# Last attention: the lower part of each head's output, formed by VectorE instead of ScalarE and GpSimd

## The chip, the cores and the metric

The kernel runs on one core of one Trainium2 chip. The metric is the device time of one execution, in microseconds; the time before is the median of 3 runs, 1202.19 us. One execution was also taken by the hardware profiler. The engines are TensorE (PE, with PEld for its weight loads), VectorE (DVE), ScalarE (ACT), GpSimd (POOL) and SyncE (SP, which issues the weight transfers).

## The reference, cut to what matters

A tensor of 256 tokens with 1024 features goes through two blocks. The second block's last layer is an attention with 8 heads of 128 features, followed by an output projection and a feed-forward part. With 256 tokens there is one block of keys, so the attention is causal softmax over all tokens:

```
h = h + moba_mixer(h, ...)        # the attention of this text
h = h + conv_ffn_2(h, ...)

def moba_mixer(x, norm_g, w_q, q_norm_g, w_o, kb, vb, kmean, cos, sin):
    q = rope(rmsnorm(rmsnorm(x, norm_g) @ w_q)) * 128 ** -0.5
    l_own = q @ k.T, masked with -inf where key > query
    p = softmax(l_own)
    o = p @ v                       # per head, 128 features
    return o.reshape(b, s, 1024) @ w_o
```

Everything is float32. The large projections must keep nearly the whole of that precision.

## The kernel before, in words

Activations lie with the features on the 128 partitions and the 256 tokens along the row (T = 256, P = 128, KD = 8 blocks of features). A projection in full float32 is replaced by three products of a rounded type (fp32r): each operand x is split into an upper part, x rounded to fp32r, and a lower part, x minus the upper part, also rounded; the product is upper times upper, lower times upper and upper times lower. Tiles seen through the rounded type carry the name `rounded` in the profile, all other tiles in the on-chip memory the name `arena`.

The weights stream through a ring of 8 slots of 8 blocks each. For each slot ScalarE writes the upper part and VectorE the lower part (`split_to`), in an order written out by hand between the other work of each engine. There is no scheduler: every engine has its own program, and semaphores join them. The accumulation banks are used in a fixed order of units; psA holds the projections and the scores of the attention (`as0` to `as7`), psB the small units: the transposed probabilities (`at0` to `at7`) and the outputs of the heads (`ao0` to `ao7`). A unit may only be opened when the unit that used its bank before has been freed (`freed`, `release`).

The last attention, for head h:

- TensorE, `scores(h)`: four products with the causal mask added as a product, into psA.
- VectorE, `a_max(h)`: two row maxima (L2427, L2428), and the negated and scaled maxima (L2430, 128x2).
- ScalarE, `a_exp(h)`: two exponentials (128 and 256 columns), each with a row sum, and the bank of the scores is free.
- VectorE: reciprocal of the sums (L2437), then the probabilities scaled in place (L2439 with 128 columns, L2440 with 256).
- TensorE, `turn(h)`: three transposes into psB (L1185). ScalarE copies them out (128x384).
- TensorE, `values(h)`: two products with the values, the output of the head, 128x256, into psB.
- ScalarE: the upper part `aoH` of the output (rounded<-psB 128x256, semaphore `ao_upper`), then a full copy `ao` of the same bank (arena<-psB 128x256), which frees the bank.
- GpSimd (L1829): `ao` minus `aoH`, in place, rounded: the lower part (semaphore `ao_rest`).

The engines are staggered. TensorE runs turn(h), values(h-1), scores(h+3) for h = 0 to 7. VectorE runs the probabilities of head h and then a_max(h+2). ScalarE runs the copy of the transposes of head h, the exponentials of head h+2, and then the two instructions on the output of head h-1.

After the heads `project_first` forms the first unit of the output projection (`bo0`): for both halves of its bank blocks 0 to 5 of the features first, then blocks 6 and 7. Before the products of block k it waits until the lower part of head k is there. Then come the other projection units and the last feed-forward part.

The helper `tt` of VectorE (L1878) issues every TENSOR_TENSOR, the helper `A` of ScalarE (L1253) every ACTIVATE, and `mm` of TensorE (L483) every product.

Of the kernel before, what the change touches and what calls it, by code (L numbers as in the profile page):

```python
# [21 lines left out]
ALU = mybir.AluOpType  # L22
# [4 lines left out]
T = 256  # L27
# [157 lines left out]
def program(nc, ins, out):  # L185
    ctx = ExitStack()
    with ctx:
# [291 lines left out]
        def _(pe):  # L479
# [75 lines left out]
            def project_first(name, src, wait, per=1):  # L555

                o = open_(name)
                assert state["blk"] == 0
                w = [[], []]
                for m in range(2):  # L560
                    w[m] = [weights(1) for k in range(KD)]
                    if m:
                        state["inc"] = False
                    for k in range(6):
                        if m == 0:
                            ready(pe, wait, k // per + 1)
                        mm3(o[:, m * T:(m + 1) * T], w[m][k], part(src, slice(0, P), k), k == 0 and m == 0, False,
                            shared=True)
                for m in range(2):
                    for k in range(6, KD):  # L570
                        if m == 0:
                            ready(pe, wait, k // per + 1)
                        elif k == 6:
                            state["inc"] = True
                        last = mm3(o[:, m * T:(m + 1) * T], w[m][k], part(src, slice(0, P), k), False, k == KD - 1,
                                   shared=True)
                close(last, name)
# [449 lines left out]
            for u in range(6, 3 * KD):  # L1027
                branch(u)
            project_first("wo0", (mgH, mg), "merged_rest")
            project([f"wo{u}" for u in range(1, 4)], (mgH, mg))  # L1030

            def ffn(f, rms):
# [18 lines left out]
                def first(j):  # L1051

                    if j == 0:
                        project_first(f"up{f}.0", GX[f"f{f}"], f"xg_f{f}")
                        sum_squares(rms, f"f{f}", GQ[f"f{f}"])
# [8 lines left out]

            project_first("lq0", GX["l"], "xg_l")
            sum_squares("r3", "l", GQ["l"])
# [80 lines left out]

            project_first("bq0", GX["b"], "xg_b")
            sum_squares("r5", "b", GQ["b"])
# [47 lines left out]
            for h in range(9):  # L1197
# [4 lines left out]
                if h < 5:  # L1202
                    scores(h + 3)
            project_first("bo0", (aoH, ao), "ao_rest")
            project([f"bo{u}" for u in range(1, 4)], (aoH, ao))
# [6 lines left out]
        def _(act):  # L1212
# [478 lines left out]
            for h in range(9):  # L1691
# [4 lines left out]
                if h:  # L1696
                    o = take(f"ao{h - 1}")[:, 0:T]
                    A(fr(aoH[:, h - 1, :]), o, ACT.Copy).then_inc(sem("ao_upper"), 1)
                    release(A(ao[:, h - 1, :], o, ACT.Copy), f"ao{h - 1}")
            ffn(2, "r6", "f1", ("bo", "x5"))  # L1700
# [5 lines left out]
        def _(pool):  # L1706
# [113 lines left out]
            for x, src in (("q", aq), ("k", ak)):  # L1820
                for u in range(4):
# [3 lines left out]
                    mul(atm[x][:, s, :], src[:, s, :], bc(cosg[x], 2)).then_inc(sem("a_cos"), 1)  # L1825
            for h in range(8):
                pool.wait_ge(*freed(f"ao{h}"))
                ready(pool, "ao_upper", h + 1)
                nc.gpsimd.tensor_tensor(fr(ao[:, h, :]), ao[:, h, :], rd(aoH[:, h, :]), ALU.subtract)\  # L1829
                    .then_inc(sem("ao_rest"), 1)  # L1830
            ffn(2, "x5")
# [3 lines left out]
        def _(dve):  # L1835
# [589 lines left out]
            def a_max(h):  # L2425
# [4 lines left out]
                V.tensor_scalar(small[:, 56 + 2 * h:58 + 2 * h], small[:, 40 + 2 * h:42 + 2 * h], -P ** -0.5,  # L2430
                                None, ALU.mult).then_inc(sem("a_max"), 1)
            a_max(0)
            a_max(1)
            for h in range(8):
# [9 lines left out]
                if h == 1:  # L2444
                    split_to(SLOT_END["bv11"] + 3)
            residual([f"bo{u}" for u in range(4)], "x5", "f2", "f1")
            ffn(2, "r6", "f1", "x_final", None, None)
# [88 lines left out]
```

## Time and profile before

| what | value |
|---|---|
| median of 3 runs (lowest, highest) | 1202.19 us (1202.01, 1202.54) |
| the profiled execution's own time | 1200.83 us |
| its span in the profile | 1198.8 us |
| TensorE busy | 1161.2 us, 97% |
| VectorE busy | 901.7 us, 75% |
| ScalarE busy | 662.6 us, 55% |
| GpSimd busy | 362.9 us, 30% |
| the last attention, from 957.0 to 977.0 us of the span: TensorE busy | 16.01 of 20.00 us |
| the same stretch: VectorE, ScalarE, GpSimd busy | 13.15, 15.17, 5.14 us |
| granted TensorE clock there | 1.00 |

The span begins with the first instruction of the profiled execution and ends with the last; the execution's own time is a little longer. A busy share over the whole span is a mean over stages of different kinds: in the projections TensorE has hardly a gap, in the attention it waits. A row in order of time has the start in the span, the duration, the engine, the line, the operation with its tiles and shapes, and in square brackets the idle time before it with what ended that. Neighbouring rows of one engine may overlap by some hundredths of a microsecond.

### The profile page before, as it was taken

To read this page: it belongs to the slowest core of one execution; us is meant where nothing else is said; L and a number is where in the kernel's file an instruction comes from. 1 tells how busy PE (TensorE), PEld (TensorE's weight loads), DVE (VectorE), ACT (ScalarE), POOL (GpSimd) and SP (SyncE) were. 2 spreads that over 40 slices of the span, in tenths; PEclk is the share of its full clock that TensorE was granted. 3 is DMA by queue.
4 is the path that set the end of the run, shared out by engine and by line. 5 is a ranking of instruction groups with operands and counts; after the bars stand their busy time and mean duration, and the time that the engine had idled before them with its cause. 6 is when DMAs were issued, how large, how long until landed. Compare 5 with 4: busy or idle time off the path is not lost.

```text
span 1198.8 us, 24765 instructions
## 1 busy us (share of the span) xinstructions
PE 1161.2 (97%) x9416; PEld 1074.1 (90%) x9416; DVE 901.7 (75%) x1305; ACT 662.6 (55%) x974; POOL 362.9 (30%) x326
## 2 busy tenths in 40 slices
PE   8999999899999999999999999999999989999998
PEld 8988678889999999989888999998898789999987
DVE  6989674456678888866757898887676768888853
ACT  5686943454445555544557565554455656555631
POOL 6634101000013555312102245550155023555400
PEclk9999999999999999999999999999999999999999
DMA  8644211236556555555432555555554325555551
GB/s 302 217 149 136 88 36 39 72 125 193 181 187 200 178 182 179 177 192 176 159 124 88 191 173 180 176 176 188 183 173 141 124 71 176 176 175 175 180 189 71
DMA packets 53987, 188.77 MB, mean 157 GB/s; under 512 B 6032, under 2 KB 6160, under 8 KB 53520
## 3 DMA queue, kind: packets, MB, share of 16 engines
q1 hardware_dynamic: 52304, 182.47, 46.9%
q10 hardware_dynamic: 1600, 5.12, 1.3%
q8 instruction: 61, 1.00, 0.3%
q14 instruction: 22, 0.18, 0.0%
HBM read 186.52 MB, written 1.05 MB: 156 GB/s over the span
## 4 chain that ended last, share of the span: by engine, by line
PE 78%; DVE 10%; ACT 7%; issue 3%; DMA 1%; POOL 0%; SPq 0%; DVEq 0%; ACTq 0%; POOLq 0%
PE psA L483 70%; PE psB L483 8%; ACT arena L1253 3%; DVE rounded L1878 3%; DVE arena L1881 3%; ACT rounded L1253 2%; DVE arena L1878 2%; ACT L1253 2%; DMA arena<-in_x 1%; DVE arena L2234 0%; DVE rounded L1881 0%; DVE arena L2389 0%; DVE arena L2330 0%; DVE arena L1912 0%; DVE arena L2283 0%
## 5 line engine op out<-in xcount | busy, mean ns | idle before, releaser
L483 PE MATMUL psA<-rounded,rounded 128*128 128x256 f32 (+1 forms) x7440 | 1011.6, 297 | 16.6 <-DVE rounded L1878 14.7
L483 PEld LDWEIGHTS psA<-rounded,rounded 128*128 128x128 f32 x7440 | 954.1, 191 | 67.3 <-issue 13.4
L1878 DVE TENSOR_TENSOR rounded<-arena,rounded 128x1024 fp32r<-128x1024 f32 (+2 forms) x362 | 458.4, 1287 | 71.6 <-ACT rounded L1253 67.8
L1253 ACT ACTIVATE rounded<-arena 128x1024 fp32r<-128x1024 f32 (+2 forms) x444 | 389.3, 922 | 184.3 <-PE psA L483 62.6
L1708 POOL TENSOR_TENSOR arena<-arena 128x256 f32<-128x256 f32 (+1 forms) x121 | 161.4, 1340 | 589.5 <-ACT arena L1253 220.9
L1253 ACT ACTIVATE arena<-arena 128x256 f32<-128x256 f32 (+6 forms) x276 | 145.4, 562 | 187.3 <-DVE arena L1878 135.1
L1881 DVE SCALAR_TENSOR_TENSOR arena<-arena 128x255 f32<-128x255 f32 (+4 forms) x338 | 177.5, 569 | 31.5 <-ACT arena L1253 21.3
L483 PE MATMUL psB<-arena 64*64 64x64 f32 (+9 forms) x1464 | 136.3, 285 | 10.1 <-DVE arena L1878 3.8
L483 PEld LDWEIGHTS psB<-arena 64*64 64x64 f32 (+4 forms) x1464 | 93.8, 152 | 41.8 <-issue 27.0
L1878 DVE TENSOR_TENSOR arena<-arena,psA 128x256 f32<-128x256 f32 (+1 forms) x84 | 38.4, 458 | 68.6 <-PE psA L483 43.4
L1795 POOL TENSOR_TENSOR rounded<-arena,rounded 128x256 f32 (+1 forms) x63 | 86.0, 1365 | 10.0 <-POOL rounded L1793 8.8
L1253 ACT ACTIVATE arena<-psA 128x512 f32<-128x512 f32 (+2 forms) x58 | 28.9, 507 | 82.8 <-PE psA L483 82.4
L1878 DVE TENSOR_TENSOR arena<-psA,arena 128x512 f32<-128x512 f32 x79 | 54.4, 690 | 20.5 <-PE psA L483 20.1
L1878 DVE TENSOR_TENSOR arena<-psB,arena 128x512 f32<-128x512 f32 (+5 forms) x63 | 34.6, 577 | 31.6 <-PE psB L483 30.7
L1253 ACT ACT_TABLE_LOAD x42 | 53.9, 1283 | 2.0 <-PEq L2530 1.2
L1253 ACT ACTIVATE arena<-psB 128x512 f32<-128x512 f32 (+4 forms) x61 | 28.6, 496 | 44.5 <-PE psB L483 40.2
L1881 DVE SCALAR_TENSOR_TENSOR rounded<-arena,rounded 128x256 fp32r<-128x256 f32 x48 | 37.9, 818 | 18.5 <-ACT rounded L1253 18.5
L1878 DVE TENSOR_TENSOR arena<-arena 128x512 f32<-128x512 f32 (+4 forms) x60 | 40.9, 694 | 11.2 <-ACT arena L1253 10.2
L1714 POOL TENSOR_TENSOR rounded<-arena,rounded 128x256 fp32r<-128x256 f32 x24 | 25.3, 1082 | 28.6 <-ACT rounded L1253 28.6
L1723 POOL TENSOR_TENSOR arena<-arena 128x512 f32<-128x512 f32 x21 | 31.6, 1505 | 1.6
L1253 ACT ACTIVATE arena<-psB,arena 128x256 f32<-128x256 f32 (+1 forms) x45 | 23.4, 562 | 15.1 <-PE psB L483 9.8
L1793 POOL CAST rounded<-arena 128x256 f32 (+1 forms) x63 | 29.0, 460 | 8.9 <-POOL arena L1708 8.0
(73 smaller groups left out, 190.9 us busy)
## 6 DMA issues: line engine op xcount, KB each, us to landing
arena<-in_w SPq DMA_DIRECT2D x343, 512.0 KB, 3.5
arena<-in_mem ACTq DMA_DIRECT2D x2, 512.0 KB, 6.4
arena<-in_x ACTq DMA_DIRECT2D x1, 1024.0 KB, 4.9
arena<-in_con ACTq DMA_DIRECT2D x1, 1024.0 KB, 5.9
out<-arena SPq DMA_DIRECT2D x1, 1024.0 KB, 3.9
arena<-in_con ACTq DMA_DIRECT2D x1, 992.0 KB, 5.1
arena<-in_w SPq DMA_DIRECT2D x2, 256.0 KB, 3.2
arena<-in_x SPq DMA_DIRECT2D x2, 256.0 KB, 5.5
```

The costliest lines, as they stand in the source:

```text
L483: ins_ = nc.tensor.matmul(o, l, r, start=start, stop=stop, skip_group_check=shared)
L1253: return nc.scalar.activation(o, i, f, **kw)
L1708: return nc.gpsimd.tensor_tensor(o, a, b, ALU.mult)
L1714: nc.gpsimd.tensor_tensor(fr(x[:, c, :]), x[:, c, :], rd(upper_[:, c, :]), ALU.subtract)\
L1723: nc.gpsimd.tensor_tensor(dst[:, 0:2, :], dst[:, 0:2, :], dst[:, c, :], ALU.add)\
L1793: nc.gpsimd.tensor_copy(hr_, gv[:, j % 2, :]).then_inc(sem("act_part"), 1)
L1795: nc.gpsimd.tensor_tensor(lr_, gv[:, j % 2, :], hi, ALU.subtract)\
L1878: return V.tensor_tensor(o, a, b, op)
L1881: return V.scalar_tensor_tensor(out=o, in0=a, scalar=s, in1=b, op0=op0, op1=op1)
```

## The change

ScalarE's full copy of each head's output goes, and GpSimd's subtraction goes. VectorE gets `ao_rest(h)`: it waits for the head's bank and for ScalarE's upper part, subtracts the upper part from the bank, writes the lower part rounded, and frees the bank. It stands in the loop over the heads at the end of turn h for head h-2, from h = 2 on, and twice behind the loop. `project_first` now takes a function that gives semaphore and value; for this projection it is the release of the head's bank, for the other three the same waits as before.

```
@@ project_first (TensorE)
-                            ready(pe, wait, k // per + 1)
+                            pe.wait_ge(*wait(k))
...
-            project_first("bo0", (aoH, ao), "ao_rest")
+            project_first("bo0", (aoH, ao), lambda k: freed(f"ao{k}"))
@@ ScalarE, loop over the heads
                 if h:
                     o = take(f"ao{h - 1}")[:, 0:T]
                     A(fr(aoH[:, h - 1, :]), o, ACT.Copy).then_inc(sem("ao_upper"), 1)
-                    release(A(ao[:, h - 1, :], o, ACT.Copy), f"ao{h - 1}")
@@ GpSimd
-            for h in range(8):
-                pool.wait_ge(*freed(f"ao{h}"))
-                ready(pool, "ao_upper", h + 1)
-                nc.gpsimd.tensor_tensor(fr(ao[:, h, :]), ao[:, h, :], rd(aoH[:, h, :]), ALU.subtract)\
-                    .then_inc(sem("ao_rest"), 1)
@@ VectorE
+            def ao_rest(h):
+                o = take(f"ao{h}")[:, 0:T]
+                ready(dve, "ao_upper", h + 1)
+                release(tt(fr(ao[:, h, :]), o, rd(aoH[:, h, :]), ALU.subtract), f"ao{h}")
             a_max(0)
             a_max(1)
             for h in range(8):
...
                 if h < 6:
                     a_max(h + 2)
                 if h == 1:
                     split_to(SLOT_END["bv11"] + 3)
+                if h > 1:
+                    ao_rest(h - 2)
+            ao_rest(6)
+            ao_rest(7)
```

How the instructions stand on VectorE, from the maxima of head 7 to the end of the loop. Before:

```order
L2427 TENSOR_REDUCE arena<-psA 128x1 [waits fullA2]
L2428 TENSOR_REDUCE arena<-psA 128x1
L2430 TENSOR_SCALAR arena<-arena 128x2 [waits dve_step]
L2437 RECIPROCAL arena<-arena 128x2 [waits freeA1]
L2439 TENSOR_SCALAR arena<-arena 128x128 [waits dve_step]
L2440 TENSOR_SCALAR arena<-arena 128x256 [waits dve_step]
L2437 RECIPROCAL arena<-arena 128x2 [waits freeA2]
L2439 TENSOR_SCALAR arena<-arena 128x128 [waits dve_step]
L2440 TENSOR_SCALAR arena<-arena 128x256 [waits dve_step]
```

And in the changed kernel, whose line numbers are 2 to 6 lower here (`psB` is the bank of a head's output, `rounded_63` the part of the memory that holds `ao` and `aoH`; `fullB` says that the output is there, `ao_upper` that ScalarE has written the upper part):

```order
L2421 TENSOR_REDUCE arena<-psA 128x1 [waits fullA2]
L2422 TENSOR_REDUCE arena<-psA 128x1
L2424 TENSOR_SCALAR arena<-arena 128x2 [waits dve_step]
L1872 TENSOR_TENSOR rounded_63<-psB,rounded_63 128x256 [waits ao_upper,fullB0]
L2435 RECIPROCAL arena<-arena 128x2 [waits freeA1]
L2437 TENSOR_SCALAR arena<-arena 128x128 [waits dve_step]
L2438 TENSOR_SCALAR arena<-arena 128x256 [waits dve_step]
L1872 TENSOR_TENSOR rounded_63<-psB,rounded_63 128x256 [waits ao_upper,fullB2]
L2435 RECIPROCAL arena<-arena 128x2 [waits freeA2]
L2437 TENSOR_SCALAR arena<-arena 128x128 [waits dve_step]
L2438 TENSOR_SCALAR arena<-arena 128x256 [waits dve_step]
L1872 TENSOR_TENSOR rounded_63<-psB,rounded_63 128x256 [waits ao_upper,fullB0]
```

The new TENSOR_TENSOR of heads 3, 4 and 5 are seen, the first two ahead of the reciprocals of heads 6 and 7.

On ScalarE, the end of the attention before (128x384 is the copy of the transposes of head 7, the rest belongs to the outputs of heads 5 to 7):

```order
L1253 ACTIVATE rounded_63<-psB 128x256 [waits fullB0]
L1253 ACTIVATE arena<-psB 128x256
L1253 ACTIVATE arena<-psB 128x384 [waits fullB1]
L1253 ACTIVATE rounded_63<-psB 128x256 [waits fullB2]
L1253 ACTIVATE arena<-psB 128x256
L1253 ACTIVATE rounded_63<-psB 128x256 [waits fullB3]
L1253 ACTIVATE arena<-psB 128x256
```

And in the changed kernel:

```order
L1253 ACTIVATE rounded_63<-psB 128x256 [waits fullB0]
L1253 ACTIVATE arena<-psB 128x384 [waits fullB1]
L1253 ACTIVATE rounded_63<-psB 128x256 [waits fullB2]
L1253 ACTIVATE rounded_63<-psB 128x256 [waits fullB3]
```

The full copies (arena<-psB 128x256) are gone; the upper parts and the copy of the transposes follow one another.

## Rows read from the trace of the kernel before

**Rows 1.** Waits between engines, 957 to 978 us: who waited for whom, total, times, longest.
```profile
PE psB L1185 <- DVE arena L2440: 3.3, 3, 1.8
```

**Rows 2.** Order of time, VectorE, 962 to 979: start, us, operation, shapes, idle before.
```profile
963.67 0.55 DVE L2439 TENSOR_SCALAR arena<-arena 128x128 f32<-128x128 f32 x1
964.25 0.35 DVE L2440 TENSOR_SCALAR arena<-arena 128x256 f32<-128x256 f32 x1
...
965.17 0.17 DVE L2430 TENSOR_SCALAR arena<-arena 128x2 f32<-128x2 f32 x1
965.25 0.16 DVE L2437 RECIPROCAL arena<-arena 128x2 f32<-128x2 f32 x1
965.45 0.29 DVE L2439 TENSOR_SCALAR arena<-arena 128x128 f32<-128x128 f32 x1
965.77 0.35 DVE L2440 TENSOR_SCALAR arena<-arena 128x256 f32<-128x256 f32 x1
967.07 0.29 DVE L2427 TENSOR_REDUCE arena<-psA 128x1 f32<-128x128 f32 x1 [0.95 <-PE psA L483]
...
967.73 0.26 DVE L2430 TENSOR_SCALAR arena<-arena 128x2 f32<-128x2 f32 x1
...
969.15 0.29 DVE L2427 TENSOR_REDUCE arena<-psA 128x1 f32<-128x128 f32 x1 [0.39 <-PE psA L483]
...
969.81 0.50 DVE L2430 TENSOR_SCALAR arena<-arena 128x2 f32<-128x2 f32 x1
...
971.89 0.74 DVE L2430 TENSOR_SCALAR arena<-arena 128x2 f32<-128x2 f32 x1
...
978.52 1.23 DVE L1878 TENSOR_TENSOR rounded<-arena,rounded 128x1024 fp32r<-128x1024 f32 x1 [4.03 <-ACT rounded L1253]
```

**Rows 3.** Order of time, GpSimd's subtractions of this attention.
```profile
963.19 0.95 POOL L1829 TENSOR_TENSOR rounded<-arena,rounded 128x256 fp32r<-128x256 f32 x1 [32.82 <-ACT arena L1253]
967.23 0.73 POOL L1829 TENSOR_TENSOR rounded<-arena,rounded 128x256 fp32r<-128x256 f32 x1 [3.09 <-ACT arena L1253]
969.56 0.73 POOL L1829 TENSOR_TENSOR rounded<-arena,rounded 128x256 fp32r<-128x256 f32 x1 [1.60 <-ACT arena L1253]
971.89 0.73 POOL L1829 TENSOR_TENSOR rounded<-arena,rounded 128x256 fp32r<-128x256 f32 x1 [1.60 <-ACT arena L1253]
```

**Rows 4.** Order of time, TensorE, the transposes of heads 2, 3, 4, 6, 7.
```profile
964.75 0.52 PE L1185 MATMUL psB<-arena 128*128 128x128 f32 x3 [1.77 <-DVE arena L2440]
...
966.87 0.49 PE L1185 MATMUL psB<-arena 128*128 128x128 f32 x3
...
968.95 0.49 PE L1185 MATMUL psB<-arena 128*128 128x128 f32 x3
...
973.56 0.52 PE L1185 MATMUL psB<-arena 128*128 128x128 f32 x3 [1.15 <-DVE arena L2440]
...
974.64 0.52 PE L1185 MATMUL psB<-arena 128*128 128x128 f32 x3
```

**Rows 5.** Order of time, ScalarE: copy of a transpose, exponential, upper part.
```profile
967.39 0.49 ACT L1253 ACTIVATE arena<-psB 128x384 f32<-128x384 f32 x1 [0.24 <-PE psB L1185]
...
972.67 0.37 ACT L1253 ACTIVATE arena<-psA,arena 128x128 f32<-128x128 f32 x1 [0.39 <-DVE arena L2430]
...
973.48 0.38 ACT L1253 ACTIVATE rounded<-psB 128x256 fp32r<-128x256 f32 x1
```

**Rows 6.** Chain that ended last, 975 to 1005 us: start, us, engine and line.
```profile
975.16 0.67 ACT arena L1253 x2
...
975.96 0.89 PE psB L483 x4
976.85 28.21 PE psA L483 x235
```

**Rows 7.** VectorE's groups by shape, whole execution: count, busy, mean ns, idle before.
```profile
L1878 DVE TENSOR_TENSOR rounded<-arena,rounded 128x256 fp32r<-128x256 f32 x11 | 4.7, 425 | 1.7 <-ACT rounded L1253 1.5
...
L1878 DVE TENSOR_TENSOR arena<-psB,arena 128x256 f32<-128x256 f32 x12 | 4.7, 421 | 4.8 <-PE psB L483 4.6
```

More of the change, by code:

```diff
@@ L571, in project_first @@
                         if m == 0:
-                            ready(pe, wait, k // per + 1)
+                            pe.wait_ge(*wait(k))
                         elif k == 6:
@@ L1028, in _ @@
                 branch(u)
-            project_first("wo0", (mgH, mg), "merged_rest")
+            project_first("wo0", (mgH, mg), lambda k: (sem("merged_rest"), k + 1))
             project([f"wo{u}" for u in range(1, 4)], (mgH, mg))
@@ L1053, in first @@
                     if j == 0:
-                        project_first(f"up{f}.0", GX[f"f{f}"], f"xg_f{f}")
+                        project_first(f"up{f}.0", GX[f"f{f}"], lambda k: (sem(f"xg_f{f}"), k + 1))
                         sum_squares(rms, f"f{f}", GQ[f"f{f}"])
@@ L1062, in _ @@
             ffn(0, "r2")
-            project_first("lq0", GX["l"], "xg_l")
+            project_first("lq0", GX["l"], lambda k: (sem("xg_l"), k + 1))
             sum_squares("r3", "l", GQ["l"])
@@ L1145, in _ @@
             ffn(1, "r4")
-            project_first("bq0", GX["b"], "xg_b")
+            project_first("bq0", GX["b"], lambda k: (sem("xg_b"), k + 1))
             sum_squares("r5", "b", GQ["b"])
```

## The prediction

> **What bounds the kernel now.** I read first the waits between engines over the last attention (957 to 978 us), then the chain of work that ended last through it, then each engine's instructions in order of time. The change touches only this stretch; every instruction ahead of it stands as it stood.
>
> The waits [rows 1] show what stops TensorE here: its transposes (L1185) wait for VectorE's scaled probabilities (L2440), 3.3 us in all. So VectorE and TensorE make one loop. I call the head h: VectorE turns head h's exponentials into probabilities (L2437, L2439, L2440); TensorE transposes them, forms the output of head h-1 and then the scores of head h+3; VectorE takes the maxima of those scores (L2427, L2428, L2430); ScalarE forms the exponentials. ScalarE's full copy and GpSimd's subtraction are not in it: the view has no engine that waits for L1829.
>
> In VectorE's own order [rows 2] the reader is to see two things. First, L2427 starts right behind TensorE's scores (idle 0.95 and 0.39 us for TensorE at 967.07 and 969.15). Second, the same instruction has two lengths. L2430 takes 0.17 us at 965.17, but 0.26, 0.50 and 0.74 at 967.73, 969.81 and 971.89. L2439 takes 0.29 at 965.45 and 0.55 at 963.67. Beside [rows 3] the cause is plain: each long one starts while a GpSimd subtraction (L1829) runs and ends 0.01 to 0.08 us or so behind it: 963.19 + 0.95 = 964.14 against 964.22; 967.96 against 967.99; 970.29 against 970.31; 972.62 against 972.63. In sum 0.26 + 0.09 + 0.33 + 0.57 = 1.25 us of VectorE's time. This is what the removed GpSimd work costs today, although nobody waits for its result.
>
> The Trainium skill (SBUF — State Buffer, "Who interferes with whom") gives the same mechanism: a VectorE tensor_scalar in a two-port mode and a GpSimd operation hold one pair of ports exclusively, and the second to come blocks until the first is done. By this rule all four stalls go and no new one comes, since GpSimd is idle in the stretch afterwards; without it the 1.25 us could not be counted on, which is a rival below.
>
> **What is removed.** Eight GpSimd subtractions: worth the stalls, as far as the loop feels them. Eight ScalarE copies of 128x256: ScalarE starts one instruction some 0.27 us later for each. ScalarE waits for the others in the loop, so seven of them I cost at nothing; what hides them is VectorE's maximum and TensorE's transpose, for which ScalarE is idle (0.39 us at 972.67, 0.24 us at 967.39 [rows 5]). The one of head 5 stands in the chain: at 975.16 [rows 6] two ScalarE instructions of 0.67 us lie between TensorE's output 6 and output 7, where the second alone is the copy that TensorE needs, 0.49 us [rows 5].
>
> **What is added.** Eight VectorE subtractions, 128x256, one operand in PSUM, one in SBUF, written as fp32r. The trace has no such form. Nearest: PSUM and SBUF in, f32 out, 421 ns; SBUF only, fp32r out, 425 ns [rows 7]. The price in the line is less than this, since an instruction that waits for nothing starts about 0.08 us before the end of the one ahead (L2437 at 965.25 starts 0.09 before L2430 ends at 965.34): 0.34 us. Bounds: nothing, where VectorE was to wait anyway; and 0.61 us, if it were as long as a 128x512 form, 0.69. I take 0.34, the two near rows agree. The Trainium skill (VectorE: DVE Perf Modes, "The TRN2 errata") would speak against the move: 120 fixed cycles for a PSUM source against 58 for SBUF, so by its figures 0.39 us here, an estimate, with 0.065 of it for reading the bank. The two rows, 421 and 425, show no such difference; by the page the sum would be 0.1 us less for the four that lie in the loop.
>
> Each subtraction also waits for ScalarE's upper part of the same head, and stands ahead of the next L2437, so that every later transpose is queued behind it. And it now releases the bank, for TensorE's output of two heads later; that output is over a microsecond away each time.
>
> **The sum, in order of time.** Steps from [rows 2, 4]: L2437 to the start of L2440 0.52 us, L2440 0.35, and 0.15 until the transpose (964.60 to 964.75); L2439 to L2440 0.32; L2427 to L2430 0.66, next 0.08 later; after L2440's start an L2427 that need not wait can come 0.27 later; transpose to the earliest next transpose 2.1 (964.75 to 966.87), transpose to the L2427 that waits for its scores 2.3 (964.75 to 967.07, 966.87 to 969.15).
> - Head 2: L2439 at 963.67 no longer stalls. L2440 at 963.99, ready 964.34, transpose at 964.49, 0.26 early. L2427 (head 4) at 964.26, L2430 964.91, subtraction 0 at 964.99, L2437 of head 3 at 965.33, ready 966.20: 0.08 late, but TensorE takes it only at 964.49 + 2.12 = 966.61, still 0.26 early.
> - Head 4: its L2427 for head 5 comes at 966.81. L2430 967.47, subtraction 1 at 967.55, L2437 967.89, ready 968.76, transpose 968.91 against 968.95. The 0.26 and the 0.09 have paid for the 0.34.
> - L2427 for head 6 at 966.61 + 2.28 = 968.89, subtraction 2 at 969.63, head 5 ready at 970.84; its transpose is again TensorE's to time. L2427 for head 7 at 968.91 + 2.29 = 971.20, L2430 at 971.86 (was 971.89), ended at 972.03 instead of 972.63.
> - Subtraction 3 at 971.94, head 6's L2437 at 972.28, ready 973.15, transpose 973.30 against 973.56.
> - Subtraction 4 must wait for ScalarE: the exponential of head 7 starts 0.04 after the maximum, at 972.07, the upper part 0.81 behind it at 972.88, done at 973.26 [rows 5]. VectorE was free at 973.07: a new wait of some 0.2 us. Head 7's L2437 follows at 973.62, ready 974.49, transpose 974.64. Before: 974.64. All the gain is spent.
> - From there ScalarE's copy starts 0.52 behind the transpose (966.87 to 967.39), at 975.16, takes 0.49, and 0.14 more go by until output 7: 975.79 instead of 975.96 [rows 6]. The projection follows 0.17 earlier.
>
> Subtractions 5 to 7 lie behind the last probabilities, beside TensorE's outputs and the first projection, which needs blocks 6 and 7 only after 36 products, over 4 us in (235 take 28.21 us [rows 6]). VectorE sits idle for 4.03 us ahead of its next weight block at 978.52 [rows 2]; the three, 1.3 us, fit in, and ScalarE reaches its part of that block sooner than before. Behind 976.85 TensorE is the chain for 28 us without a gap, so what the projection gains or loses is handed on whole.
>
> So -0.2 us on the profiled execution: 1200.83 (span 1198.8 and 2.0 around it) to 1200.65; the median of the runs stood 1.36 higher, at 1202.19, so 1202.0.
>
> **Rivals.**
> - *The stalls stay.* VectorE's slow instructions could have another cause than GpSimd. For: only coincidence in time shows it. Against: four of four, to 0.08 us. Then head 4 becomes ready 0.34 later (969.11, transpose 0.3 late), L2427 for head 7 at 971.55, and subtractions 3 and 4 are paid too: transpose 7 about 0.9 late, less 0.17: +0.7 us, 1202.9. It stays within 0.2%.
> - *The subtractions are hidden.* If VectorE had room everywhere, TensorE would time all of it: transposes 0.26 early to head 5, head 6 gets the stall of 0.57 on top, and head 7 is 0.85 early: with the 0.17 -1.0 us, 1201.2. Against it: VectorE's idle time in the loop is 0.95 and 0.39 us ahead of the heads 5 and 6 [rows 2], and ahead of head 7's L2427 there is no idle time that could hide a subtraction.
> - *All removed work counts*: 1.25 us and eight times 0.27: -3.4 us, 1198.8. Only if ScalarE were the bound; its idle times speak against.
> - *VectorE is tied to ScalarE in every head* (the slower side). Subtraction h-2 waits for an upper part that ScalarE does only behind an exponential. If that were the exponential of the same turn, each of four turns would cost 0.04 + 0.81 + 0.38 + 0.34 = 1.6 us between maximum and next probabilities, 6.3 in all less 1.25 saved: +5 us, 1207. It decides from the point at which the upper part comes later than the maximum of head h+2. By the order it belongs to the exponential of the turn before, done 0.5 to 0.9 us ahead for subtractions 0 to 3 (upper part of head 3 before at 971.15, subtraction at 971.94); only subtraction 4 is caught.
>
> **Numbers.** About 0.2% (2.4 us) is what a measurement can tell from no change. The forecast, -0.6 to +0.4 us, has 0.66. Stalls stay (or a subtraction of 0.61 us): 0.14. Hidden: 0.12. All removed work: 0.04. Tied to ScalarE: 0.04. Time 1202.0; the range from 1201.0 to 1203.3 takes in the hidden case and the staying stalls, with the long subtraction. Faster 0.04, within 0.92, slower 0.04.
>
> **What would show it.** Right: L2430 and L2439 at 0.17 and 0.29 in all eight heads; subtractions of about 0.42 us, the fifth with a wait of some 0.2 us for ScalarE; transposes early by up to 0.3 us for heads 2 to 6 and level for head 7; in the chain, output 7 at 975.8 and the projection at 976.7 instead of 975.96 and 976.85. Wrong: a long L2430 with GpSimd idle; a wait for ScalarE ahead of subtractions 0 to 3; TensorE waiting in the projection's first 16 blocks for a subtraction; a difference that arises before 963 us or behind 977.

## The result, and the profile after

The changed kernel is slower: 1203.96 us against 1202.0 us, medians of 20 runs each, ratio 1.0018 with a 95% interval of 1.0012 to 1.0025. (One execution of 3956.55 us is left out of the ratio; without it the median is 1203.86.) The forecast of 1202.0 stood for no change, with a range from 1201.0 to 1203.3 and 0.04 for a slower kernel: wrong, by about 2 us. The 20 runs of before reach from 1198.58 to 1203.62, so the three shown at first, 0.5 us apart, told too little of its spread.

The attention first. A row of the changed kernel stands some 1 us later than its counterpart of before, from a difference that was there already at head 1's transpose (961.78 against 960.71). So each transpose is measured here from head 1's:

| head | 2 | 3 | 4 | 5 | 6 | 7 | projection |
|---|---|---|---|---|---|---|---|
| before, us | 4.04 | 6.16 | 8.24 | 10.52 | 12.85 | 13.93 | 15.90 |
| after, us | 3.78 | 5.89 | 8.19 | 10.30 | 12.59 | 14.00 | 15.84 |
| difference | -0.26 | -0.27 | -0.05 | -0.22 | -0.26 | +0.07 | -0.06 |
| forecast | -0.26 | -0.26 | -0.04 | -0.20 | -0.26 | 0 | -0.17 |

(The forecast of head 5 is worked out here: one step of 2.12 us behind head 4's 968.91 is 971.03, against 971.23.)

VectorE, order of time, the changed kernel, 964 to 980 (start, us, operation, idle before):

```profile
964.74 0.29 DVE L2437 TENSOR_SCALAR arena<-arena 128x128 f32<-128x128 f32 x1
...
968.53 0.17 DVE L2424 TENSOR_SCALAR arena<-arena 128x2 f32<-128x2 f32 x1
968.61 0.42 DVE L1872 TENSOR_TENSOR rounded<-psB,rounded 128x256 fp32r<-128x256 f32 x1
...
970.62 0.17 DVE L2424 TENSOR_SCALAR arena<-arena 128x2 f32<-128x2 f32 x1
...
972.94 0.17 DVE L2424 TENSOR_SCALAR arena<-arena 128x2 f32<-128x2 f32 x1
973.02 0.42 DVE L1872 TENSOR_TENSOR rounded<-psB,rounded 128x256 fp32r<-128x256 f32 x1
973.36 0.15 DVE L2435 RECIPROCAL arena<-arena 128x2 f32<-128x2 f32 x1
...
974.43 0.42 DVE L1872 TENSOR_TENSOR rounded<-psB,rounded 128x256 fp32r<-128x256 f32 x1 [0.21 <-ACT rounded L1253]
974.77 0.15 DVE L2435 RECIPROCAL arena<-arena 128x2 f32<-128x2 f32 x1
...
979.26 1.23 DVE L1872 TENSOR_TENSOR rounded<-arena,rounded 128x1024 fp32r<-128x1024 f32 x1 [0.45 <-ACT rounded L1253]
```

L2424 is L2430 of [rows 2], L2437 is L2439. The four stalls of [rows 2] (0.55, 0.26, 0.50, 0.74) are 0.29, 0.17, 0.17, 0.17. A subtraction takes 0.42 us and costs 0.34 in the line (973.02 to 973.36); the fifth waits 0.21 us for ScalarE. Before the first four nothing is waited for: each starts 0.78 us or more behind the end of its upper part. TensorE's transposes and the chain, as [rows 4] and [rows 6]:

```profile
961.78 0.52 PE L1185 MATMUL psB<-arena 128*128 128x128 f32 x3 [0.36 <-DVE arena L2438]
965.56 0.52 PE L1185 MATMUL psB<-arena 128*128 128x128 f32 x3 [1.50 <-DVE arena L2438]
...
975.78 0.52 PE L1185 MATMUL psB<-arena 128*128 128x128 f32 x3 [0.24 <-DVE arena L2438]
```

```profile
974.43 0.42 DVE rounded L1872
...
976.97 0.89 PE psB L483 x4
977.86 28.21 PE psA L483 x235
```

The fifth subtraction is now a link of the chain. The projection's 28.21 us without a gap are those of [rows 6].

Then the last feed-forward part. Its first half has a loop of 16 units (four passes of a body of four). In a unit VectorE reads a full bank (psA, 128x512), writes a lower part of weights (rounded, 128x1024), does the taps of the convolution (two of 128x255, two of 128x254, shown as four of 128x255 in order of time) and writes a second lower part; ScalarE forms the gate (two of 128x256) and two upper parts; GpSimd multiplies (arena, 128x256), rounds the product (CAST) and subtracts for its lower part. Up to this loop's entry at 1031 us the changed kernel lies 1.01 us behind; at 1131 us it lies 3.45 behind. Groups of VectorE and GpSimd in the loop, by shape (count, busy, mean ns, idle before); before, 1036 to 1125:

```profile
L1878 DVE TENSOR_TENSOR rounded<-arena,rounded 128x1024 fp32r<-128x1024 f32 x31 | 40.9, 1319 | 0.1
L1881 DVE SCALAR_TENSOR_TENSOR arena<-arena 128x255 f32<-128x255 f32 x30 | 16.3, 583 | 2.9 <-ACT arena L1253 2.4
...
L1795 POOL TENSOR_TENSOR rounded<-arena,rounded 128x256 f32 x15 | 22.5, 1498 | 2.8 <-POOL rounded L1793 2.8
...
L1793 POOL CAST rounded<-arena 128x256 f32 x15 | 6.0, 398 | 2.5 <-POOL arena L1708 2.5
```

The changed kernel, 1037 to 1126:

```profile
L1872 DVE TENSOR_TENSOR rounded<-arena,rounded 128x1024 fp32r<-128x1024 f32 x30 | 36.6, 1220 | 0.1
L1875 DVE SCALAR_TENSOR_TENSOR arena<-arena 128x255 f32<-128x255 f32 x30 | 20.7, 728 | 6.1 <-ACT arena L1253 6.1
...
L1792 POOL CAST rounded<-arena 128x256 f32 x15 | 20.6, 1376 | 2.5 <-POOL arena L1707 2.5
L1794 POOL TENSOR_TENSOR rounded<-arena,rounded 128x256 f32 x15 | 13.2, 879 | 2.8 <-POOL rounded L1792 2.8
```

The same instructions, with other lengths: the CAST 1376 ns instead of 398, the taps 728 instead of 583, but a weight block 1220 instead of 1319 and GpSimd's subtraction 879 instead of 1498. The wait that matters has turned round; waits of before (who waited for whom, total, times, longest):

```profile
DVE arena L1878 <- PE psA L483: 3.2, 15, 0.2
```

and of the changed kernel:

```profile
PEld psA L483 <- DVE rounded L1872: 3.4, 14, 0.4
PE psA L483 <- DVE rounded L1872: 0.5, 3, 0.2
```

In each of 15 units VectorE waited some 0.2 us for TensorE's bank; now TensorE waits for VectorE's weights. How it begins stands in order of time. GpSimd before:

```profile
1035.97 1.30 POOL L1708 TENSOR_TENSOR arena<-arena 128x256 f32<-128x256 f32 x1 [3.58 <-ACT arena L1253]
1037.44 0.40 POOL L1793 CAST rounded<-arena 128x256 f32 x1 [0.17 <-POOL arena L1708]
1038.02 1.50 POOL L1795 TENSOR_TENSOR rounded<-arena,rounded 128x256 f32 x1 [0.18 <-POOL rounded L1793]
...
1043.34 0.40 POOL L1793 CAST rounded<-arena 128x256 f32 x1 [0.17 <-POOL arena L1708]
```

VectorE before:

```profile
1031.14 0.69 DVE L1878 TENSOR_TENSOR arena<-psA,arena 128x512 f32<-128x512 f32 x1 [0.63 <-PE psA L483]
...
1033.41 1.90 DVE L1881 SCALAR_TENSOR_TENSOR arena<-arena 128x255 f32<-128x255 f32 x4
...
1036.90 0.69 DVE L1878 TENSOR_TENSOR arena<-psA,arena 128x512 f32<-128x512 f32 x1 [0.23 <-PE psA L483]
1037.51 1.41 DVE L1878 TENSOR_TENSOR rounded<-arena,rounded 128x1024 fp32r<-128x1024 f32 x1
```

GpSimd in the changed kernel:

```profile
1038.73 1.25 POOL L1792 CAST rounded<-arena 128x256 f32 x1 [0.17 <-POOL arena L1707]
1040.17 0.74 POOL L1794 TENSOR_TENSOR rounded<-arena,rounded 128x256 f32 x1 [0.18 <-POOL rounded L1792]
...
1044.72 1.43 POOL L1792 CAST rounded<-arena 128x256 f32 x1 [0.17 <-POOL arena L1707]
```

VectorE in the changed kernel:

```profile
1032.15 0.69 DVE L1872 TENSOR_TENSOR arena<-psA,arena 128x512 f32<-128x512 f32 x1 [0.65 <-PE psA L483]
...
1034.70 1.90 DVE L1875 SCALAR_TENSOR_TENSOR arena<-arena 128x255 f32<-128x255 f32 x4 [0.24 <-ACT arena L1253]
...
1037.91 0.69 DVE L1872 TENSOR_TENSOR arena<-psA,arena 128x512 f32<-128x512 f32 x1
1038.51 1.22 DVE L1872 TENSOR_TENSOR rounded<-arena,rounded 128x1024 fp32r<-128x1024 f32 x1
```

From the first read of the bank to the taps it is 2.27 us before (1031.14 to 1033.41) and 2.55 after (1032.15 to 1034.70), since ScalarE's gate starts 1.02 behind that read before (1032.16) and 1.31 after (1033.46), 0.29 late. In the next unit the CAST comes 0.07 ahead of the weight block before (1037.44, 1037.51), and takes 0.40; after, the weight block is first (1038.51, 1038.73), and the CAST takes 1.25: it ends at 1039.98, 0.25 behind the block's end at 1039.73. GpSimd's subtraction then falls on the taps. A unit takes 5.90 us before (CAST to CAST, 1037.44 to 1043.34) and 5.98 to 6.04 after, each fourth 6.16 to 6.19. The loop's first CAST comes 0.30 us later behind the one ahead of it than before (6.57 against 6.27), the 15 steps from there to the end of the loop 2.15: 2.4 us in all. With the 0.06 gained in the attention this is 2.3 us, beside 2.2 by the ratio (1.4 to 3.0).

The rest of the profiles' difference, 1.0 us, is there before the attention and is not laid to the change, since the code is the same in both kernels up to there. By VectorE's reads of full banks 0.5 us of it is there at 345 us, at a granted clock of 1.00 in both executions; between 494 and 662 us it rises to 1.17. In that stretch the granted clock stood at 1.00 (2.4 GHz) in the one execution, and at 1.2 GHz for 3.4 us from 658.9 on in the other; TensorE was busy for 5.50 us of the 8 from 652 to 660 in both. The same 3.4 us stand near 660 us in the traces of `before104`, `late29` and `late25` of the next section, which have the attention of before. Before (us, busy and count of PE, PEld, DVE, ACT, POOL, granted clock):

```profile
660.00:680.00 20.00, 18.82 (x157) 18.64 (x156) 16.43 (x26) 9.83 (x15) 7.30 (x7) 1.00 0.61 210
```

After:

```profile
660.00:680.00 20.00, 19.53 (x154) 19.36 (x153) 15.40 (x24) 8.95 (x14) 6.22 (x6) 0.94 0.62 191
```

### The profile page after: what moved, and what is told of

Same layout as the page of the kernel before. It is cut to its first block, busy times and chain, and to the rows that moved or that the text cites. A ratio compares the mean times of both kernels' runs of the same rounds, so it can differ in the third digit from the quotient of the medians.

```text
span 1202.2 us, 24757 instructions
## 1 busy us (share of the span) xinstructions
PE 1164.5 (97%) x9416; PEld 1076.0 (89%) x9416; DVE 903.8 (75%) x1313; ACT 659.1 (55%) x966; POOL 361.9 (30%) x318
## 4 chain that ended last, share of the span: by engine, by line
PE 76%; DVE 12%; ACT 7%; issue 3%; DMA 1%; POOL 0%; SPq 0%; DVEq 0%; ACTq 0%; POOLq 0%
PE psA L483 67%; PE psB L483 8%; DVE rounded L1872 4%; DVE arena L1875 4%; ACT arena L1253 4%; ACT rounded L1253 2%; DVE arena L1872 2%; ACT L1253 2%; DMA arena<-in_x 1%; DVE arena L2228 0%; POOL arena L1707 0%; DVE rounded L1875 0%; PE psB L1185 0%; DVE arena L2383 0%; DVE arena L1906 0%
## 5 line engine op out<-in xcount | busy, mean ns | idle before, releaser
L1875 DVE SCALAR_TENSOR_TENSOR arena<-arena 128x255 f32<-128x255 f32 (+4 forms) x338 | 181.7, 581 | 35.1 <-ACT arena L1253 25.6
L1794 POOL TENSOR_TENSOR rounded<-arena,rounded 128x256 f32 (+1 forms) x63 | 76.7, 1218 | 10.0 <-POOL rounded L1792 8.8
L1253 ACT ACTIVATE arena<-psB 128x512 f32<-128x512 f32 (+4 forms) x53 | 25.6, 511 | 47.1 <-PE psB L483 40.3
L1792 POOL CAST rounded<-arena 128x256 f32 (+1 forms) x63 | 43.6, 692 | 8.9 <-POOL arena L1707 8.0
```

Of the source, the lines that this page charges most:

```text
L1253: return nc.scalar.activation(o, i, f, **kw)
L1792: nc.gpsimd.tensor_copy(hr_, gv[:, j % 2, :]).then_inc(sem("act_part"), 1)
L1794: nc.gpsimd.tensor_tensor(lr_, gv[:, j % 2, :], hi, ALU.subtract)\
L1875: return V.scalar_tensor_tensor(out=o, in0=a, scalar=s, in1=b, op0=op0, op1=op1)
```

## The experiments

The theory: ScalarE's loop code now lies 8 instructions earlier, its first gate comes 0.29 us late by that place alone, and the late gate turns the order of CAST and weight block for the whole loop. "Place" is the number of the loop's first instruction in ScalarE's program, counted from the trace's records with a loop's body counted once, modulo 128: 67 before, 59 after.

**The eight instructions back, as short copies.** `pad8` is the changed kernel with

```
                 A(fr(aoH[:, h - 1, :]), o, ACT.Copy).then_inc(sem("ao_upper"), 1)
+                A(small[:, 97 + h:97 + h + 1], par[:, 0:1], ACT.Copy)
```

> The changed kernel, with eight ScalarE copies of one column (128x1, scratch) where the eight full copies of 128x256 stood; all else of the change stays. ScalarE's later instructions stand again where they stood before the change. Theory A (place of ScalarE's code): ScalarE enters the last up loop 0.3 us late in the changed kernel only because its code lies 8 instructions earlier; here the entry is not late (gap from ScalarE's last register operation to its first ACTIVATE under 0.1 us, as before), GpSimd's CAST takes 0.40 us in all loop turns, a unit takes 5.90 us, and the time is 0 to 0.4 us under the kernel before (ratio 0.9997 to 1.000). Theory B (the attention's new order shifts the phase of the engines): the code place does not matter; the loop stays at 6.03 us a unit, ratio 1.0018. Theory C (chance between executions): no fixed relation, ratio between.

1202.31 us against 1202.55, ratio 0.9998 (0.9989 to 1.0007). GpSimd in its loop, 1039 to 1128:

```profile
L1793 POOL CAST rounded<-arena 128x256 f32 x15 | 6.0, 397 | 2.5 <-POOL arena L1708 2.5
```

The loss is gone though the attention still is the changed one. What it needs is eight more instructions, 128x1 each, not their work.

**The place in the kernel before.** `before120` has the attention of before, and 120 such copies far ahead, so that the loop lies at place 59:

```
@@ gained(), ScalarE
+                    if tag == "b" and u < 7:
+                        for n in range(18 if u == 0 else 17):
+                            A(cst("posI")[:, 18 * u + n:18 * u + n + 1], par[:, 0:1], ACT.Copy)
```

> The kernel before, untouched in the attention; 120 ScalarE copies of one column are added beside the second feed-forward part's down products (18 after the first unit, 17 after each of the next six). The code of the last up loop then starts at the same place modulo 128 instructions as in the changed kernel (128 instructions are one of the 8 KB instruction loads in the transfer records). Theory A: ScalarE is 0.3 us late at the entry of the last loop, GpSimd's CAST takes 1.25 to 1.44 us, a unit about 6.03 us from there on; 2.3 us more in the loop, ratio about 1.002 (less if the ring gives something back, more by up to 1 us if the copies delay weight blocks). Theory B: the loop runs at 5.90 us a unit, ratio 1.000 to 1.0005.

1204.23 us against 1202.55, ratio 1.0017 (1.0008 to 1.0026), a unit 6.02 us:

```profile
L1796 POOL CAST rounded<-arena 128x256 f32 x15 | 20.6, 1376 | 2.5 <-POOL arena L1711 2.5
```

So the loss comes with none of the change. `before104`, the same with 14 or 15 copies a unit (place 43), tells the place from the number of copies:

> The kernel before with 104 ScalarE copies of one column beside the second feed-forward part's down products (14, then six times 15), as in before120: the last loop's code starts at place 43 modulo 128, on the other side of 59. Theory A with one boundary crossed by the loop's first instructions: at 43 the entry is in time and the units take 5.90 us; if it is late, every place in the lower half of an 8 KB block is bad and not only the one near 59. It also shows what the added copies cost by themselves, since before120 differs from it by 16 of them.

One execution: 1202.43 us, CAST 397 ns on the mean. The number of copies is not what does it.

**Eight copies early.** `early8` is the changed kernel with eight pads in `gate_of`, so that all three loops lie 8 further back (67, 121, 67):

```
@@ ScalarE, for u in range(6, 3 * KD)
+                if u < 14:
+                    A(small[:, 92 + u:92 + u + 1], par[:, 0:1], ACT.Copy)
```

> The changed kernel, with eight ScalarE copies of one column between the branch merges of the first block, ahead of all three up loops. By theory A all three loops' code now starts at places (67, 121 and 67 modulo 128) at which no late entry was seen; the first loop, late in both kernels (CAST 1.24 us once, 6.56 us from the fourth to the fifth unit), enters in time (6.27 us) and the last too: ratio 0.9995 to 0.9999, 0.2 to 0.6 us under the kernel before. Theory B: as the changed kernel, 1.0018.

1202.68 us against 1202.55, ratio 1.0003 (0.9995 to 1.0012). The loops do what was expected, the first one too, whose first CAST now comes ahead of the weight block (`early8`, GpSimd):

```profile
401.31 0.40 POOL L1794 CAST rounded<-arena 128x256 f32 x1 [0.17 <-POOL arena L1709]
```

where every other kernel has 1.24 or 1.25 us. The expected gain on the whole is not seen in the time; it would be below what 12 runs tell.

**Four and two copies behind the attention.** `end4` (place 63) and `end2` (place 61) are the changed kernel with N = 4 or 2 copies just ahead of the last feed-forward part:

```
+            for n in range(N):
+                A(cst("posI")[:, n:n + 1], par[:, 0:1], ACT.Copy)
             ffn(2, ...)
```

> The changed kernel, with four ScalarE copies of one column behind the attention, ahead of the last feed-forward part: its loop's code starts at place 63 modulo 128, between 59 (late in four cases of four) and 67 (in time in three of three). By theory A the entry is either late by 0.29 us with slow units, or in time with 5.90 us a unit, nothing in between; it narrows the place of the step. By theory B it stays slow wherever the code lies.

> The changed kernel with two ScalarE copies of one column behind the attention: the last loop's code starts at place 61 modulo 128, between 59 (late in all cases) and 63 (in time in the run end4). Either the entry is late by 0.29 us or not at all; if late, slow units to the end. The step lies between two neighbouring places, so both are open; what theory A excludes is an entry late by another amount.

One execution each: `end4` 1203.44 us, CAST 398 ns, a unit 5.90; `end2` 1205.7 us, CAST 1377 ns, slow to the end. Two more instructions of 128x1 decide. (The 1203.44 of `end4` shows how little one execution's time says by itself; its loop is the fast one.)

**Lateness by itself, in the kernel before.** If it is the lateness and not the place that turns the order, a delay of ScalarE at the loop's entry must do the same. The copies stand behind a wait for the bank that the gate follows, so that they delay it:

```
@@ ScalarE, first(j)
+                    if f == 2 and j == 3:
+                        act.wait_ge(sem(f"freeA{a0 % 4}"), 1 + a0 // 4 + 1)
+                        A(cst("posI")[:, 0:P], par[:, 0:P], ACT.Copy)
```

This is `late_entry`; `late2` has one copy of 128x256, `late24` and `late33` two and three of 128x1.

> The kernel before, with one added ScalarE copy of 128x128 between the fourth unit of the last up phase and its loop, behind the same wait as the loop's first ACTIVATE, so that this ACTIVATE starts some 0.27 us late without any change of the attention. It separates the late entry from all else. Theory A, second half (a late entry alone tips the order of GpSimd's CAST and VectorE's weight block, and the loop stays there): the CAST takes 1.25 to 1.44 us for most units, 6.03 us a unit, 2.3 us more, ratio 1.0018 to 1.002. Rival (the entry's delay is taken up within one or two units, as in the first feed-forward part's loop, which enters late in both kernels and recovers): 0.1 to 0.4 us, ratio 1.0002.

> The kernel before, with the entry of the last loop delayed as in the run late_entry, by a copy of 128x256 in place of 128x128: some 0.35 us late, a little more than the 0.29 us of the changed kernel, with ScalarE's code one instruction further than before. Theory A1 (lateness of this size is all it takes): GpSimd's CAST is long in nearly every unit, 6.03 us a unit, 2.3 us more than before: ratio 1.0015 to 1.002. Rival A2 (the loop takes a late entry up within two or three units, as it did in late_entry and as the first loop does in every kernel; what keeps it slow is something in the loop that goes with the place of ScalarE's code, beyond the entry): ratio 1.0002 to 1.0005, CAST at 0.40 us from the third unit on.

> As late33, with two copies: 0.24 us late, below the 0.29 us of the changed kernel. A1: slow units of 6.02 us to the end, or, if the threshold lies between 0.24 and 0.29 us, recovery after two or three units; A2: recovery here and in late33.

> The kernel before; at the entry of the last loop three ScalarE copies of one column behind the wait of the loop's first ACTIVATE. One such copy makes the entry 0.15 us late (run late_entry), each further one takes 0.09 us: 0.33 us late, a little over the 0.29 us of the changed kernel, without its place of the code. Theory A1 (a late entry of 0.3 us alone is what keeps the loop slow, 0.15 us was too little): GpSimd's CAST 1.25 to 1.45 us in nearly all units, 6.02 us a unit, ratio 1.0015 to 1.002. Rival A2 (the loop recovers after two or three units whatever the lateness): ratio 1.0003 to 1.0006, CAST 0.40 us from the third or fourth unit on.

| kernel | time, us | beside, us | ratio | taps behind first read, us | CAST |
|---|---|---|---|---|---|
| before | | | | 2.27 | 0.40 |
| late_entry | 1203.58 | 1202.55 | 1.0007 (0.9998 to 1.0016) | 2.42 | two long, then 0.40 |
| late2 | 1202.71 | 1202.03 | 1.0006 (0.9997 to 1.0015) | 2.42 | the same |
| late24 | 1201.93 | | one execution | 2.42 | the same |
| late33 | 1201.95 | 1201.84 | 1.0001 (0.9992 to 1.0010) | 2.42 | the same |

All four missed the lateness that they were built for, and all are late by the same 0.15 us. ScalarE's sequencer does its register operations for the loop behind the new wait: in `late33` the gate starts 0.44 us behind the wait's end, against 0.29 from the bank's release to the gate before. These copies run beside the register operations and are hidden; the 0.15 us is the longer row of operations. GpSimd in `late33`:

```profile
1037.82 1.40 POOL L1797 CAST rounded<-arena 128x256 f32 x1 [0.17 <-POOL arena L1712]
...
1043.96 1.28 POOL L1797 CAST rounded<-arena 128x256 f32 x1 [0.17 <-POOL arena L1712]
...
1049.85 0.40 POOL L1797 CAST rounded<-arena 128x256 f32 x1 [0.17 <-POOL arena L1712]
```

Two units are slow, then the loop finds back. Two larger delays followed: `late29` with copies of 128x1 and 128x448, `late25` with one of 128x512.

```
+                        A(con2[:, 600:601], par[:, 0:1], ACT.Copy)
+                        A(con2[:, 0:448], par[:, 0:448], ACT.Copy)
```

> The kernel before; at the entry of the last loop ScalarE runs a copy of one column and one of 128x448, so long that the loop's first ACTIVATE is held back past its register operations: 0.28 to 0.30 us late, as in the changed kernel, with the code two instructions beyond its place of before. A1 (lateness alone decides): GpSimd's CAST is long in nearly every unit, 6.02 us a unit, ratio 1.0015 to 1.002. A2 (something that goes with the place of the code is needed beyond the entry): CAST at 0.40 us from the third or fourth unit on, ratio 1.0002 to 1.0006.

> As late29 with one copy of 128x512: 0.25 us late. A1: slow units to the end if the threshold lies between 0.15 and 0.25 us, else recovery; A2: recovery.

`late29`: 1204.17 us against 1202.21, ratio 1.0014 (1.0005 to 1.0023); the taps stand 2.53 us behind the first read (1033.45 to 1035.98), 0.26 late. `late25`, one execution: 1204.31 us, taps 2.50 behind, 0.23 late. Both are slow to the end of the loop, `late29` with GpSimd's groups of the changed kernel:

```profile
L1797 POOL CAST rounded<-arena 128x256 f32 x15 | 20.7, 1377 | 2.5 <-POOL arena L1712 2.5
L1799 POOL TENSOR_TENSOR rounded<-arena,rounded 128x256 f32 x15 | 13.2, 880 | 2.8 <-POOL rounded L1797 2.8
```

With ScalarE's code at a place that enters in time (69 and 68 in these two), the delay alone makes the whole loss. Between 0.15 and 0.23 us lies the point from which this loop does not recover. It is no rule for every loop of this body: the loop of the first feed-forward part, at place 59 in all kernels but `early8`, is some 0.3 us late too (taps 2.57 us behind the read, 2.29 in `early8`), and only its first CAST is long.

**Forcing the order.** If the weight block's being first is the harm, VectorE might wait for the CAST. `forced` is the changed kernel with

```
+                    if f == 2:
+                        ready(dve, "act_part", u * 2 + f * (UPS - 1) * 2)
                     split_one(s0 + 2 * j + 3, ...)
```

> The changed kernel; in the last feed-forward part VectorE waits, ahead of the weight block that follows the read of a unit's bank, until GpSimd's CAST of the unit before is done. ScalarE's code stands where the changed kernel has it, so its entry is 0.3 us late here too. Theory (the slow loop is the order of these two: GpSimd's CAST queued behind VectorE's 1.22 us weight block): with the order forced the CAST takes 0.40 us in all units and a unit 5.90 us behind the first; the time is that of the kernel before or 0.2 to 0.5 us above it (VectorE waits 0.2 us where it was blocked 0.2 us), ratio 1.000 to 1.0005. Rival (the late entry costs 2 us by itself, whatever the order, or VectorE's added wait costs as much as it saves): 1.0015 to 1.002, a unit 6.0 us.

1207.06 us against 1202.03, ratio 1.0041 (1.0027 to 1.0054): a miss. VectorE and GpSimd in its loop, 1038 to 1127:

```profile
L1872 DVE TENSOR_TENSOR rounded<-arena,rounded 128x1024 fp32r<-128x1024 f32 x30 | 36.8, 1226 | 10.8 <-POOL rounded L1792 9.9 <-issue 0.4
...
L1792 POOL CAST rounded<-arena 128x256 f32 x15 | 6.0, 399 | 2.5 <-POOL arena L1707 2.5
```

The CAST is short again, but VectorE pays 9.9 us of waiting for it, and a unit takes 6.16 to 6.51 us: the wait costs more than the order gives.

**GpSimd's work back, beside the new subtractions.** `pool_dead` is `pad8` with eight subtractions of GpSimd into memory that nobody reads, each released by the upper part:

```
+            for h in range(8):
+                ready(pool, "ao_upper", h + 1)
+                nc.gpsimd.tensor_tensor(atm["k"][:, h, :], rd(aoH[:, h, :]), rd(aoH[:, h, :]), ALU.subtract)
```

> The kernel of the run pad8 (ScalarE's code in its old place), with eight GpSimd subtractions 128x256 on the heads' upper parts, whose results nobody reads, waiting for each upper part. It measures what the prediction called the rival of the staying stalls: VectorE's subtractions and GpSimd's port use together. Port theory: wherever GpSimd's subtraction runs, L2437, L2438 or L2424 of the changed numbering becomes long again (0.3 to 0.7 us in place of 0.17 to 0.35); the transpose of head 7 and the output projection come 0.3 to 1.0 us later than in pad8, counted from the transpose of head 2. Rival (the long instructions before had another cause): lengths as in pad8, no shift.

1201.6 us in one execution. Counted from head 2's transpose, as it was expected, the projection comes at the same time in both (12.05 us): a miss. From head 1's transpose it is 15.99 us against 15.83 in `pad8`, since the only long VectorE instruction lies ahead of head 2's; VectorE:

```profile
964.41 0.44 DVE L2441 TENSOR_SCALAR arena<-arena 128x128 f32<-128x128 f32 x1
```

GpSimd:

```profile
963.65 1.12 POOL L1828 TENSOR_TENSOR arena<-rounded 128x256 f32<-128x256 f32 x1 [32.56 <-ACT rounded L1253]
```

The others come 0.3 to 0.6 us earlier than those of [rows 3], and run beside VectorE's row maxima and new subtractions, which read the banks and keep their lengths (0.29, 0.41 to 0.42, and 0.42 to 0.43 us). So the cost, 0.16 us, is one stall, and the four stalls of [rows 2] were each due to what VectorE did at that moment.

## Why the prediction was wrong, by its steps

- *The stalls are GpSimd's and go.* Held: 0.29 and 0.17 everywhere. The Trainium skill (SBUF — State Buffer, "Who interferes with whom"), which has the shared ports as an exclusive lock, agrees with that, and with the loop, where the CAST that starts behind the weight block ends 0.25 us behind it. *The stalls stay* fell.
- *The price of a subtraction, 0.34 in the line.* Held: 0.42 us each, 0.34 from one start to the next. On the mean the eight took 424 ns, against 425 from SBUF [rows 7]. The Trainium skill (VectorE: DVE Perf Modes, "The TRN2 errata") has 120 cycles for a PSUM source against 58; no such difference is seen.
- *The walk through the heads.* Held to 0.07 us for each transpose, the new wait of 0.21 us ahead of subtraction 4 as well. *Hidden* fell, since they were paid for in the line; *Tied to ScalarE* fell, since subtractions 0 to 3 waited for nothing.
- *The projection 0.17 earlier.* Mis-sized: 0.06. From head 7's transpose to output 7 it is 1.19 us (975.78 to 976.97) instead of 1.32 (974.64 to 975.96 in [rows 4, 6]): 0.13 gained rather than 0.17, since the copy started 0.56 and not 0.52 behind the transpose (975.78 to 976.34); and head 7's transpose had lost 0.07.
- *Seven of the ScalarE copies cost at nothing.* In time they do. But with the eighth they are eight instructions of a program, and this step put at nothing, without a reason, that whatever ScalarE does behind them moves by eight places. This is the failed step: it measured 2.4 us in the last feed-forward part, against a gain of 0.06 in the attention. `pad8`, `end2`, `end4`, `before120` and `before104` show it by place; `late29` and `late25` show how an entry 0.23 to 0.26 us late becomes 2 us.
- *Behind 976.85 TensorE is the chain, what the projection gains or loses is handed on whole.* Held up to the loop at 1031 us, 54 us on. It was read from the 28 us after the attention and taken for the rest. In the loop VectorE had only 0.2 us a unit to spare before TensorE waits for it, and no row of it was looked at. The prediction's own list named "a difference that arises behind 977" as a sign of error, and this is it.
- The range had no case for code far behind the change: all rivals were mechanisms of the attention.

What stays open, and how far the records lead. ScalarE makes one pause of 0.29 us with nothing waited for, and in each kernel below at a number of its program that is 64 modulo 128:

| kernel | place | pause between | us there, us without | number, modulo 128 |
|---|---|---|---|---|
| changed | 59 | last register operation and gate | 0.40, 0.10 | 1088, 64 |
| before120 | 59 | the same | 0.38, 0.10 | 1216, 64 |
| end2 | 61 | two register operations, two instructions earlier | 0.38, 0.08 | 1088, 64 |
| end4 | 63 | the loop's first two instructions | 0.35, 0.06 | 1088, 64 |

In `end4` ScalarE then waits another 2.06 us for VectorE's bank, so the pause costs nothing; at 59 and 61 it lies behind that wait, and the gate is late by all of it. At 67 it lies ahead of the loop, at 43 beside a running ACTIVATE, at 113 and 121 not in the loop at all. At the numbers that are 0 modulo 128 there is none (`early8`, 768: 0.08 us in all four passes of its loop), so the period is 128, not 64 or 32.

ScalarE's instructions are loaded in blocks, and a change of block at that number fits. The page of the profile, before and after, has for such loads

```profile
q8 instruction: 61, 1.00, 0.3%
q14 instruction: 22, 0.18, 0.0%
```

which is 16 KB and 8 KB a piece. In all 16 traces a load of 8 KB on q14 starts 2.1 to 2.7 us after ScalarE comes to the number 448, ahead of or in its first loop (1033.10 and 1035.53 for the number 1088 in the changed kernel). No run changed the loading, so that the pause is the change of block is argued and not shown. The Trainium skill (Runtime: NRT & Kernel Launch, "Instruction fetch mechanics") holds that a block is 16 KiB and that crossing into the next is mostly hidden; the loads on q14 are half of that here, and a crossing was worth 0.29 us at one place and 2 us in the end. Nor was it shown why the first loop recovers from its late entry within one unit; its next gate stands 0.07 us earlier behind the read of its bank than in the last loop (0.94 against 1.01).

No version beats the kernel before: `pad8` and `early8` have intervals that hold 1.

## What to carry to other kernels

Adding or removing instructions on an engine moves all its later code. Where a tight loop follows, look at its first pass: an entry that is 0.3 us late for no wait is the sign, and a few 128x1 instructions ahead of the loop show by experiment whether place is the cause (here four were enough, and two were not). Before a local gain is "handed on whole", read the slack of each later stage, and which two engines share a port there with starts only hundredths of a microsecond apart: such a pair has two orders, and a small push can change it for the whole loop.

## What was not expected of the hardware

- One loop, the same instructions, two steady rhythms: 5.90 us a unit with the CAST ahead, 5.98 to 6.04 and each fourth 6.16 to 6.19 with the weight block ahead. A push of 0.15 us is forgotten after two units, one of 0.23 us not before the loop ends.
- 0.29 us at a loop's entry from the place of ScalarE's code alone, late at 59 and 61, in time at all others, in every kernel run; the pause sits at one number of the program, 64 modulo 128, and moves through the loop's entry as instructions are added ahead of it.
- The VectorE subtraction that reads one operand from a bank keeps its 0.42 us beside a running GpSimd subtraction (`pool_dead`), where a scaling of probabilities grows from 0.29 to 0.44.
- Two instructions of 128x1 (`end2` to `end4`) stand between the two rhythms.
- Removing eight copies from ScalarE, seven of them off the chain, made the kernel slower by 2 us.
